# Square buffers, late sums and a few additions on another engine, in a fused two-block kernel

## The reference, cut to what matters

```python
# end of each of the four parts: y is the output of the last projection
x = x + gate * rms_norm(y, g_post)         # post-norm and residual
h = rms_norm(x, g_pre) * (1 + sc) + sh     # pre-norm of the next part (sc, sh in the first block)
z = h @ w_next

def rms_norm(x, gain):
    return x * rsqrt(mean(x * x, axis=-1) + eps) * gain
```

## Time and profile before

| | |
|---|---|
| median of 3 runs | 3016.02 us (3013.66 to 3024.22) |
| profiled execution | 3020.56 us, span 3018.8 us, mean granted TensorE clock 0.962 |
| TensorE busy | 2816.0 us, 93% |
| VectorE busy | 1228.2 us, 41% |
| ScalarE busy | 854.6 us, 28% |
| GpSimd busy | 867.0 us, 29% |
| chain that ended last | TensorE 83%, VectorE 7%, ScalarE 3%, no visible cause 3%, GpSimd 2% |

### The profile page before, as it was taken

The page is one execution under the profiler, slowest core; times in us unless marked ns, Lnnn a source line. Parts: engine busy times, 40 slices in busy tenths (PEclk is TensorE's granted clock), DMA queues, the critical chain, the costliest instruction groups (busy, mean ns, idle before and its releaser), DMA issues.

```text
span 3018.8 us, 31426 instructions
## 1 busy us (share of the span) xinstructions
PE 2816.0 (93%) x13134; PEld 2184.7 (72%) x13134; DVE 1228.2 (41%) x1572; ACT 854.6 (28%) x1288; POOL 867.0 (29%) x412
## 2 busy tenths in 40 slices
PE   6888889799999999978999999999879999999996
PEld 3656647588888888757777777777667888888875
DVE  6646612565435353455656422221443112111115
ACT  4413643332212121234453221111343112222112
POOL 1322113334334242342111121111244333333333
PEclk8999999899999999988999999999989999999998
DMA  5453254211111111312113121111312111111113
GB/s 225 178 132 97 64 209 165 105 42 56 42 49 45 47 54 45 108 67 98 43 49 105 56 79 53 53 52 52 125 63 98 49 49 56 49 49 40 45 49 140
DMA packets 84845, 240.22 MB, mean 80 GB/s; under 512 B 10592, under 2 KB 25440, under 8 KB 84704
## 3 DMA queue, kind: packets, MB, share of 16 engines
q1 hardware_dynamic: 76672, 213.48, 20.5%
q10 hardware_dynamic: 4608, 14.92, 1.3%
q0 software_dynamic: 3424, 9.81, 0.9%
HBM read 201.63 MB, written 36.54 MB: 79 GB/s over the span
## 4 chain that ended last, share of the span: by engine, by line
PE 83%; DVE 7%; ACT 3%; issue 3%; DMA 2%; POOL 2%; SPq 1%; ACTq 0%; POOLq 0%; DVEq 0%
PE ps L1265 24%; PE ps L1266 23%; PE ps L1267 23%; PE pc L1621 3%; PE pss L1571 1%; POOL whl L2794 1%; PE pss L1234 1%; PE ps L1482 1%; DVE y L1639 1%; PE ps L1428 1%; PE ps L1303 1%; DMA adaw<-in_w_ada 1%; DVE y L1645 1%; ACT act L2358 1%; POOL y L2794 1%
## 5 line engine op out<-in xcount | busy, mean ns | idle before, releaser
L2794 POOL TENSOR_TENSOR whl<-wraw,whl 128x1024 fp32r<-128x1024 f32 (+1 forms) x238 | 617.2, 2596 | 1647.7 <-ACT whl L2358 1647.5
L1265 PE MATMUL ps<-act,whl 128*128 128x512 f32 x2464 | 1000.8, 406 | 42.4 <-DVE act L1645 10.0
L1266 PE MATMUL ps<-act,whl 128*128 128x512 f32 x2464 | 973.3, 395 | 0.0
L1267 PE MATMUL ps<-act,whl 128*128 128x512 f32 x2464 | 972.9, 395 | 0.0
L1265 PEld LDWEIGHTS ps<-act,whl 128*128 128x128 f32 x2464 | 469.4, 191 | 185.7 <-issue 72.0
L1266 PEld LDWEIGHTS ps<-act,whl 128*128 128x128 f32 x2464 | 469.8, 191 | 105.8 <-issue 8.9
L1267 PEld LDWEIGHTS ps<-act,whl 128*128 128x128 f32 x2464 | 468.7, 190 | 103.8
L1265 PE MATMUL ps<-hid,whl 128*128 128x512 f32 x864 | 343.9, 398 | 20.4 <-issue 11.6
L1266 PE MATMUL ps<-hid,whl 128*128 128x512 f32 x864 | 341.8, 396 | 0.0
L1267 PE MATMUL ps<-hid,whl 128*128 128x512 f32 x864 | 339.1, 393 | 0.0
L2358 ACT ACTIVATE whl<-wraw 128x1024 fp32r<-128x1024 f32 (+1 forms) x238 | 246.7, 1037 | 300.7 <-PE ps L1267 274.0
(11 more groups left out here) (302 smaller groups left out, 2481.0 us busy)
## 6 DMA issues: line engine op xcount, KB each, us to landing
wraw<-in_w_in SPq DMA_DIRECT2D x60, 512.0 KB, 3.5
wraw<-in_f1u SPq DMA_DIRECT2D x44, 512.0 KB, 3.5
wraw<-in_f2d SPq DMA_DIRECT2D x36, 512.0 KB, 3.4
wraw<-in_w_out SPq DMA_DIRECT2D x32, 512.0 KB, 3.5
x<-in_w_ada SPq DMA_DIRECT2D x32, 512.0 KB, 6.6
wraw<-in_f2u SPq DMA_DIRECT2D x32, 512.0 KB, 3.4
xs<-y SPq DMA_DIRECT2D x24, 512.0 KB, 3.4
x<-in_xT ACTq DMA_DIRECT2D x16, 512.0 KB, 8.8
```

The costliest lines, as they stand in the source:

```text
L1265: pe.matmul(PSB[g.bank][:, :], hi, src[:, 0, k, c], start=e == 0, stop=False)
L1266: pe.matmul(PSB[g.bank][:, :], hi, src[:, 1, k, c], start=False, stop=False)
L1267: m = pe.matmul(PSB[g.bank][:, :], lo, src[:, 0, k, c], start=False, stop=e == len(ks) - 1)
L2794: return g_.tensor_tensor(out, a, b, op)
```

## The change

Four edits belong together.

- The ring of square buffers has three places in s=1, 2 and 4, and still two in s=5. For it, `tmp` has three buffers instead of four in s=1 and s=4 and the memory behind it is laid out anew; in s=2 a buffer `late` is added.
- `norm_add` no longer puts all pending sums ahead of its own steps; a pending sum is put only where its buffer is about to be used again (`use_sq`).
- In `residual` the sum of panel j-1 is put behind the addition and square of panel j, the pause per panel is 2.2 us in half 0 and 1.8 us in half 1 instead of 1.4 us, and half 0 has another 1.0 us ahead of `r_rows2`.
- In half 0 of s=5 all eight additions of x are on GpSimd.

```diff
     def use_sq(self, s, label):
 
-        ring = self.sq.setdefault(s, [0, [None, None]])
-        b = ring[0] % 2
+        size = 2 if s == 5 else 3
+        ring = self.sq.setdefault(s, [0, [None] * size])
+        b = ring[0] % size
         ring[0] += 1
+        self.add_sums(lambda entry: entry[3] == b)
         free = ring[1][b]
         ring[1][b] = label
         return b, free
 
-    def add_sums(self):
-
-        while self.sums:
+    def add_sums(self, due=lambda entry: True):
+
+        while any(map(due, self.sums)):
             self.put("r_sum", *self.sums.pop(0))
 
     def norm_add(self, s, half, j, t):
-        self.add_sums()
         b, free = self.use_sq(s, ("nd", s, half, j))
         self.put("nadd", s, half, j, b, free, t)
...
-            yield 1.4
-            p.add_sums()
+            if j:
+                p.add_sums(lambda entry: entry[2] < j)
+            yield 1.8 if half else 2.2
             if len(sums) > 1:
                 p.put("r_sum", s, half, *sums.pop(0))
         if final:
             return
         yield 1.0
+        p.add_sums()
         if half:
             p.put("r_sum", s, half, *sums.pop(0))
+        else:
+            yield 1.0
         p.put("r_rows2", s, half)
...
-            sqb[s] = [sb(f"sq{s}{b}", [P, 512], c=c)[:, :] for b in range(2)]
-            tmp[s] = [sb(f"tm{s}{b}", [P, 512], c=c)[:, :] for b in range(4)]
-            sb(f"over{s}", [P, 3096], c=c)
+            sqb[s] = [sb(f"sq{s}{b}", [P, 512], c=c)[:, :] for b in range(3)]
+            tmp[s] = [sb(f"tm{s}{b}", [P, 512], c=c)[:, :] for b in range(1)]
+            sb(f"over{s}", [P, 1024 + 3096], c=c)
+            tmp[s] += [sb(f"tn{s}{b}", [P, 512], c=c)[:, :] for b in range(2)]
...
+        def add_on_pool(s, half, j):
+            return j % 2 == 1 or (s == 5 and half == 0)
+
         def added_done(s, half, j):
-            return done("raP" if j % 2 else "raD", s, half, j)
+            return done("raP" if add_on_pool(s, half, j) else "raD", s, half, j)
```

More of the change, by code:

```diff
@@ L1080, in build @@
         diag[2] = sb("diag2", [P, 512], c=c4)[:, :]
+        late = sb("late", [P, 512], c=c4)[:, :]
         c4.close()
@@ L1084, in build @@
         ss[2] = pad[2]
-        sqb[2] = [cv[:, 512 * h:512 * h + 512] for h in range(2)]
+        sqb[2] = [cv[:, 512 * h:512 * h + 512] for h in range(2)] + [late]
         pb2 = ExitStack()
@@ L2000, in r_add @@
                     *mark("raD", "t", s, half, j))
-                if j % 2 == 0:
+                if not add_on_pool(s, half, j):
                     w.wait_ge(*x_done(s, j))
@@ L2855, in r_add @@
             def r_add(s, half, j):
-                if j % 2:
+                if add_on_pool(s, half, j):
                     c = HALF[half]
```

## The result

The changed kernel takes 3009.03 us (median of 9 runs, 3005.36 to 3014.06), the kernel before beside it 3021.56 us (9 runs): ratio 0.9961, 95% interval 0.9949 to 0.9973, 12 us or 0.4% faster. The profiled execution's span goes from 3018.8 to 3005.6 us. Forecast was a gain of 17.2 us, 2999 us, with a range of 2988 to 3012. Direction and range hold; of the gain, 12.5 us are there and a good quarter is missing. (Over its nine runs the kernel before has a median 5.5 us above the 3016.02 of three runs that the forecast started from, so gains are compared here, not end times. The prediction's own line for "faster", 3007, was drawn from the old median: the end time misses it, the gain of 12.5 us is over its 9.)

The account below looks back on a forecast made before the run. TensorE, busy 93% of the span, was taken as the bound, improvable only in its waits and the slow clock behind them. Terms 3.3 + 3.7 + 7.5 + 2.7 = 17.2 us gave 2999 us from the median 3016.02; range 2988 to 3012.

Parts of the forecast that it names:

- Places in the queues: Longer pauses in the planner let TensorE reach first-half `r_rows2` 6.8 us later, with that much more matmul work done.
- The price of a tile behind `apply`: s=1: two tiles instead of three evicted behind first-half `apply`, 2.10 us each; second half's last sum about 4.4 us earlier.
- 6.8 of these 9 us are only moved: s=1: TensorE's wait shrinks from 15.35 to about 6.4 us, but 6.8 us of that is idle shifted elsewhere.
- The loop: s=1 and s=4: odd square to odd square over three engines takes 7.15 us instead of 9.20, through GpSimd's split.
- The rival built on it: VectorE and GpSimd block each other: loop 11.1 us, s=1 and s=4 cost 8.4 us each, total 3030; chance 0.07.
- s=1 and s=4: Late sums, third square buffer and later places gain 3.3 us (2.1 to 4.4) and 3.7 us (2.1 to 4.5).
- s=2: Down-projection stage: long waits for weights and the 6.27 us wait with its slow tail disappear; gain 7.5 us (3 to 9.5).
- with no slow clock, the half ends near 1329: s=2: four waits of 1.3 to 2.3 us left, matmuls end near 1329 instead of 1342, next projection near 1341.
- 8 panels x 2.72 no longer fit into its 32.6 us: s=2: first-half `r_rows2`, `r_bc2` and `apply` fall behind the last matmul; waits of 3.6, 4.0 and 2.2 us.
- s=5: Four even additions moved from VectorE to GpSimd save 3.2 us, less about 0.5 for one stretched sum; net 2.7 (1.5 to 4.5).
- `tmp` at three buffers: s=1 and s=4: scaling waits for the subtraction three panels back; taken as 0, at most 2.1 us without cover.
- moved, not removed: Rival: loop stays near 7.9 us, s=1, s=4 and s=2 give nothing, s=5 stays; gain 3 to 6 us, 3011; chance 0.18.

Follow-up runs that it names:

- 7: Changed kernel with first-half `r_rows2` put 2.7 us further on in s=1 and s=4; ratio to the kernel before 0.9931.
- 10: Also spelled before_later_rows2: kernel before with only first-half `r_rows2` put 9.5 us further on in s=1 and s=4; ratio to the kernel before 0.9970.
- 3: Changed kernel with two square buffers in every stage, pauses and late sums kept; ratio to the kernel before 0.9975.
- 4: Changed kernel with s=2 alone at 1.8 us pauses and without the additional 1.0 us; ratio to the kernel before 0.9976, s=2 129.0 us.
- 1: Also spelled s5_adds_only: kernel before with all eight first-half additions of s=5 on GpSimd; one run, 3025.9 us against 3022.2, s=5 24.5 us.

## Why the prediction was right, and where its sizes were off

**Places in the queues.** Forecast: `r_rows2` reached 6.8 us later, waits of about 6.4 us there and 5 to 6 us before the second half's rows. Measured: reached 7.0 us later, waits of 7.35 and 5.92 us (7.37 and 3.84 in s=4). The price of a tile behind `apply` (2.10 us) was the right term, as 7 confirms. That "6.8 of these 9 us are only moved" holds for the idle at `r_rows2`, but 10 shows that moving it is itself worth 3.6 to 5.2 us when it takes tiles out from behind `apply`.

**The loop.** The mis-sized term is 7.15 us. It is 7.49: its last step, "addition to square 1.32", is 1.79, because GpSimd's addition waits for VectorE's held sum (two other steps are 0.1 us shorter together). The prediction had VectorE as the loser only ("no row shows GpSimd stretched by a sum"), and priced the sum beside the split at nothing. That reading holds for the rows shown, not for the trace of the kernel before, which has the same 0.46 us on a split. GpSimd, where a split is 2.39 us, then VectorE, held by the split ahead of it:

```profile
569.28 2.85 POOL L2794 TENSOR_TENSOR whl<-wraw,whl 128x1024 fp32r<-128x1024 f32 x1
```

```profile
568.06 1.81 DVE L1639 TENSOR_TENSOR ss<-ss,sq 128x512 f32<-128x512 f32 x1 [1.40 <-ACT sq L2358]
```

So the price of the block could have been read before the change was built. The first odd square came at 521.01 (520.3 forecast, 0.4 of it an offset at the stage's start), the last at 543.40 (541.8). The Trainium skill says in SBUF — State Buffer, section "Who interferes with whom", that whoever issues first blocks the other; here the trace agrees in both directions, 2.68 us for VectorE's 0.69 and 1.76 for GpSimd's 1.29. The rival built on it (each blocking added to a 9.2 us loop, 3030 us) was far too dear: the block hides behind the split but for its last 0.45 us.

**s=1 and s=4.** Forecast 3.3 and 3.7. Measured 2.4 and 3.4 in the profiles shown (1.9 and 3.4 by means), and another 1.1 us in the stretch behind s=1, which the prediction had not looked at. There the clock comes back earlier behind waits of the same length: windows of TensorE from 0.5 us behind the matmul that ends the stage, kernel before, then changed.

```profile
604.00:607.00 3.00, 3.00 (x8) 0.50 0.00 0
607.00:610.00 3.00, 3.00 (x9) 0.57 0.00 0
```

```profile
602.10:605.10 3.00, 3.00 (x8) 0.50 0.00 0
605.10:608.10 3.00, 3.00 (x14) 0.96 0.00 0
```

The stretch from there to the start of s=2 is 655.3 us in both profiles with the old s=1 and 653.8 to 654.7 in the twelve others, so it goes with what was altered in s=1. Of that, the later place of `r_rows2` is enough: it is all that before_later_rows2 alters, with 654.0 us. How it reaches past the end of the stage no run shows.

**s=2.** Forecast 7.5 (3 to 9.5), measured 5.6 in the profiles shown, 4.9 by means. The predicted waits are there: 1.38, 1.78, 1.75 and 2.50 for weights (1.3 to 2.3 forecast), 1.84 for the last sum (3.6), diagonal 4.47 (4.0), first applied panel 2.32 (2.2); no wait at the second half's rows, and its broadcast at 1352.1, or 1355.1 with the stage's start 3.0 us earlier (1353 to 1356). What failed is "with no slow clock, the half ends near 1329": `r_rows2` is reached at 1329.58, which is 1332.6 on the old time scale, and the next projection starts at 1344.3, not 1341. The clock falls before the half ends, in the first windows below, which an estimate from them puts at 1.6 us (half of the 1.44 us from 1322.36 on, then 4 x 0.22); the other 2 us of the 3.6 aren't taken apart. The clock falls again with the open chain: that "the new idle brings the clock down" was the lower bound's condition, not the forecast's.

```profile
1319.80:1323.80 4.00, 1.50 (x5) 0.79 0.12 32
1323.80:1327.80 4.00, 4.00 (x15) 0.78 0.62 228
1327.80:1331.80 4.00, 2.16 (x12) 1.00 0.01 2
1331.80:1335.80 4.00, 0.67 (x6) 0.57 0.29 89
1335.80:1339.80 4.00, 2.07 (x2) 0.50 0.47 173
1339.80:1343.80 4.00, 2.47 (x6) 0.50 0.01 4
```

That "8 panels x 2.72 no longer fit into its 32.6 us" is right only with what comes ahead of them: the eight are 21.8 us, 12 steps (8.2 us) pass before the first addition and 2.7 us follow the last, 32.6 in all, so `r_rows2` just misses the half. 3 and 4 say, by one profile each, that this stage needs both the buffer and the pauses.

**s=5.** Forecast 2.7, measured 2.1; the difference is one more stretched sum (1). The Trainium skill's advice in GPSIMD Engine Reference, section "Engine selection", to keep such additions on VectorE as about twice as fast (1.28 against 0.69 here) did not decide it: GpSimd stood idle for 1.3 to 1.7 us before six of the eight additions, and was never late.

**`tmp` at three buffers.** Priced at nothing. It wasn't tried alone; from its first scaling to its last operation VectorE's part of `apply` takes 11.1 us in s=1 and 8.3 in s=4, before and after.

**The sum.** 2.4 + 3.4 + 5.6 + 2.1 = 13.5 in the stages; with 1.1 gained behind s=1 and 0.9 lost between s=2 and s=4 and 0.4 before s=1, 13.3 of the profile's 13.2. That these others nearly cancel is chance: the stretch between s=2 and s=4 alone runs from 810.2 to 816.3 us in the fourteen profiles. By gain the forecast (17.2) is nearer to the 12.5 measured than "moved, not removed" (3 to 6), whose mechanism is not what happened either: s=1 and s=4 did give, and s=2 kept most of its gain.

## What to carry to other kernels

Before shortening the chain that an engine waits for, ask what stands behind the waiting step in the other engines' queues: moving the step past two more evictions gave at least as much in s=1 and s=4 as the whole change, and both together (0.993) beat either. Count a block between VectorE and GpSimd to its end in both directions: the one held does its work when the other is done, and what then starts on the first engine waits for it. And check where a moved step lands against transfers: at the end of the queue it stood behind a weight panel still on its way.

## What the runs showed of the hardware

- A VectorE addition of 8 columns, started beside a GpSimd operation of 2.40 us, took 2.15 us and ended 0.02 us behind it; alone it takes 0.17 us. A full sum of 512 columns ended 0.56 us behind the same operation, so what is held adds its own work behind the end, and the wait before that is the same.
- GpSimd is held too: its addition took 1.76 us instead of 1.29 where VectorE's held sum still had 0.56 us to do behind the split.
- The granted clock behind much the same wait differs from execution to execution, with the code of the stage unchanged. In s=2 the kernel before has 0.50 in each of the two windows of 4 us that begin with the return from a wait of 7.73 us and 0.81 in the third, with TensorE busy throughout; s5_adds_only has 0.62 in the first and 1.00 in the second behind 9.34 us. The stage differs by 3 us, as much as a part of this change gives.
